# A hybrid decoder trunk on one Trainium2 core: the loads, row scales and last column pair of its first phase rearranged

## The reference, cut to what matters

```python
def rms_norm(t, gain):
    y = t32 * lax.rsqrt(jnp.mean(t32 * t32, axis=-1, keepdims=True) + NORM_EPS)
    return (y * gain).astype(t.dtype)

def modulate(h, shift, scale):
    return h * (1.0 + scale[:, None, :]) + shift[:, None, :]

c_act = jax.nn.silu(c)
mod = c_act @ ada_w[layer] + ada_b[layer]               # 2048 x 12288, six sections
h = modulate(rms_norm(x, norm_g[layer, 0]), shift_t, scale_t)
qkv = (h @ w_qkv).reshape(bsz, seq, N_A_GROUPS, 3, A_HEADS, HEAD_DIM)
q = apply_rope(rms_norm(qkv[:, :, g, 0], q_gain[g]), cos, sin)
```

## Time and profile before

| | |
|---|---|
| time before, median of 3 runs | 2384.81 us |
| lowest and highest | 2383.89 and 2385.09 us |
| span of the profiled execution, first to last instruction | 2381.5 us |
| mean granted TensorE clock | 0.998 |
| TensorE busy | 2340.9 us (98%) |
| VectorE busy | 1781.9 us (75%) |
| ScalarE busy | 1265.2 us (53%) |
| GpSimd busy | 52.8 us (2%) |
| moved by DMA | 665.38 MB, mean 279 GB/s |

### The profile page before, as it was taken

The page is one execution under the profiler, slowest core; times in us unless marked ns, Lnnn a source line. Parts: engine busy times, 40 slices in busy tenths (PEclk is TensorE's granted clock), DMA queues, the critical chain, the costliest instruction groups (busy, mean ns, idle before and its releaser), DMA issues.

```text
span 2381.5 us, 28881 instructions
## 1 busy us (share of the span) xinstructions
PE 2340.9 (98%) x11309; PEld 1933.7 (81%) x11309; DVE 1781.9 (75%) x2291; ACT 1265.2 (53%) x2162; POOL 52.8 (2%) x74
## 2 busy tenths in 40 slices
PE   7999999999999999999999999999999999999999
PEld 4478888887888888888887878877888888888887
DVE  6677888878999888789787887868875555555554
ACT  3166566667535535535546666654653553543552
POOL 1000000001000000000001210000100000000000
PEclk9999999999999999999999999999999999999999
DMA  9987888967999888898896877757886555555555
GB/s 391 424 324 288 320 296 311 359 220 256 356 390 345 336 307 327 299 337 315 315 350 224 324 305 249 264 179 288 302 282 194 189 192 194 186 194 193 187 191 172
DMA packets 151000, 665.38 MB, mean 279 GB/s; under 512 B 17392, under 2 KB 17872, under 8 KB 121424
## 3 DMA queue, kind: packets, MB, share of 16 engines
q1 hardware_dynamic: 150864, 663.53, 76.0%
HBM read 661.33 MB, written 2.13 MB: 279 GB/s over the span
## 4 chain that ended last, share of the span: by engine, by line
PE 82%; DMA 7%; DVE 6%; ACT 3%; issue 1%; POOL 1%; SPq 0%; ACTq 0%; DVEq 0%
PE main L512 18%; PE main L426 15%; PE main L428 15%; PE main L427 15%; PE main L514 9%; DMA qT<-ada 3%; DMA ada_raw<-ada 2%; DVE w_lo L1312 2%; DVE ada_raw L1319 2%; PE main L440 2%; PE main L442 2%; PE main L441 2%; DMA w_raw<-w 1%; ACT w_hi L885 1%; DVE qT L1319 1%
## 5 line engine op out<-in xcount | busy, mean ns | idle before, releaser
L885 ACT ACTIVATE w_hi<-w_raw 128x1024 fp32r<-128x1024 f32 x771 | 809.8, 1058 | 802.7 <-DMA w_raw<-w 798.6
L1312 DVE TENSOR_TENSOR w_lo<-w_raw,w_hi 128x1024 fp32r<-128x1024 f32 x771 | 933.9, 1224 | 398.1 <-ACT w_hi L885 392.0
L1319 DVE CUSTOM_DVE_ANT_0 ada_raw<-ada_raw,c_row,biasc 128x2048 f32<-128x2048 f32 x208 | 492.6, 2368 | 52.2 <-DMA ada_raw<-ada 50.4
L512 PE MATMUL main<-hT,w_hi 128*128 128x512 f32 x1856 | 464.7, 392 | 0.0
L512 PEld LDWEIGHTS main<-hT,w_hi 128*128 128x128 f32 x1856 | 334.3, 189 | 60.1
L426 PE MATMUL main<-w_hi,mid_hi 128*128 128x512 f32 x960 | 373.9, 389 | 1.0 <-DVE w_lo L1312 1.0
L427 PE MATMUL main<-w_lo,mid_hi 128*128 128x512 f32 x960 | 373.6, 389 | 0.0
L428 PE MATMUL main<-w_hi,mid_lo 128*128 128x512 f32 x960 | 373.5, 389 | 0.0
L426 PE MATMUL main<-w_hi,hT 128*128 128x512 f32 x848 | 338.9, 400 | 1.5 <-DVE hT L1478 1.0
L428 PE MATMUL main<-w_hi,hT 128*128 128x512 f32 x848 | 330.9, 390 | 0.0
L427 PE MATMUL main<-w_lo,hT 128*128 128x512 f32 x848 | 330.1, 389 | 0.0
(11 more groups left out here) (270 smaller groups left out, 1772.8 us busy)
## 6 DMA issues: line engine op xcount, KB each, us to landing
w_raw<-w SPq DMA_DIRECT2D x800, 512.0 KB, 4.3
ada_raw<-ada SPq DMA_DIRECT2D x208, 1024.0 KB, 7.1
qT<-ada SPq DMA_DIRECT2D x16, 1024.0 KB, 12.3
gate<-gate_rows SPq DMA_DIRECT2D x4, 1024.0 KB, 7.7
xs<-x SPq DMA_DIRECT2D x1, 2048.0 KB, 7.7
out<-xs SPq DMA_DIRECT2D x3, 512.0 KB, 6.7
out<-xs SPq DMA_DIRECT2D x2, 256.0 KB, 2.5
st_a<-lamb SPq DMA_DIRECT2D x1, 256.0 KB, 18.2
```

Source lines behind the costliest of these rows:

```text
L512: pe.matmul(banks[f][:, :], w_hi[:, s, wc], hT[:, :, kt, :], start=(kt == 0), stop=False)
L885: act.activation(w_hi[:, s, :], w_raw[:, s, :], ACT.Copy).then_inc(hi_done, 1)
L1312: dve.tensor_tensor(w_lo[:, s, :], w_raw[:, s, :], w_hi[:, s, :].bitcast(F32), ALU.subtract).then_inc(lo_done, 1)
L1319: dve.tensor_tensor_reduce(piece, piece, c_row[:, :], gain, biasc[:, section, kt:kt + 1], ALU.mult, ALU.add, out).then_inc(ada_used, 1)
```

## The change

1. The loads of `cols_in` and `biasc` are issued by ScalarE instead of SP, so that `x` is SP's first.
2. `x_recip` stands ahead of the second dot instead of behind it. ScalarE runs a square root on one element of `gate` early, between the exponential of `c` and its first copies.
3. One more weight piece is issued ahead of `pos_i` and `lamb`; every later one stands one place earlier. In the last pair's group the order is ada, w, ada, w, ada, w, ada, w, and two w follow.
4. In the last pair the four `ada` pieces are reordered: shift and scale of k-tile 14, then shift and scale of k-tile 15. ScalarE modulates and copies by k-tile (`last_high`), VectorE subtracts by k-tile (`last_low`), and TensorE runs all four parts for k-tile 14, then all four for k-tile 15 (`last_pair`).
5. The last two pieces of the seventh pair (j = 6) are multiplied in parts as well (`FIRST_EARLY` = 2).

```diff
 FIRST_SPLIT = 3
+FIRST_EARLY = 2
+FIRST_HALVES = PIECES + PK - 1
 ADA_QKV = [((g, c), j) for g, c, js in (
...
 
-            sp.dma_start(cols_in[0:96, :], vecs_in).then_inc(vec_in, 16)
-            sp.dma_start(biasc[:, :, :], bias_cols_in).then_inc(bias_in, 16)
             sp.dma_start(xs[:, :, :], x_in.rearrange("(t p) d -> p t d", p=P)).then_inc(x_in_done, 16)
...
                 first_ada(a)
+            weight_piece()
             weight_piece()
...
                     weight_piece()
-                for a in range(2, FIRST_PIECES):
-                    first_ada(FIRST_PIECES * j + a)
+                first_ada(FIRST_PIECES * j + 2)
+                if j == PIECES - 1:
+                    weight_piece()
+                first_ada(FIRST_PIECES * j + 3)
+                if j < PIECES - 1:
+                    weight_piece()
                 weight_piece()
-                weight_piece()
-            for _ in range(FIRST_CHUNKS - 1):
+            for _ in range(FIRST_CHUNKS - 2):
                 weight_piece()
...
                 banks = (main[0], main[1], (sc, ov), tr)[part]
-                if j == PIECES - 1 and part != first_order(j)[0]:
-                    pe.wait_ge(hT_split, PIECES)
+                if j == PIECES - 2 and part in first_order(j)[-FIRST_EARLY:]:
+                    pe.wait_ge(hT_split, j + 1)
                     s = next_piece()
                     for k in range(PK):
                         for t in range(T):
                             kt, tc, wc = PK * j + k, cols(t, P), cols(k, NC)
                             pe.matmul(banks[t][:, :], hT_hi[:, kt, tc], w_hi[:, s, wc], start=False, stop=False)
                             pe.matmul(banks[t][:, :], hT_hi[:, kt, tc], w_lo[:, s, wc], start=False, stop=False)
-                            last = pe.matmul(banks[t][:, :], hT_lo[:, kt, tc], w_hi[:, s, wc], start=False,
-                                             stop=(k == PK - 1))
+                            last = pe.matmul(banks[t][:, :], hT_lo[:, kt, tc], w_hi[:, s, wc], start=False, stop=False)
                     last.then_inc(mm_done, 1)
...
                         last = pe.matmul(banks[t][:, :], stb[:, j % 2, cols(k * T + t, P)], w_raw[:, s, cols(k, NC)],
-                                         start=(j == 0 and k == 0), stop=(j == PIECES - 1 and k == PK - 1))
+                                         start=(j == 0 and k == 0), stop=False)
                 last.then_inc(mm_done, 1)
+
+            def last_pair():
+
+                j = PIECES - 1
+                fills, raw = divmod(n["w"].n, SLOTS)
+                n["w"].up()
+                slots = [raw]
+                for k in range(PK):
+                    kt, wc = PK * j + k, cols(k, NC)
+                    for i, part in enumerate(first_order(j)):
+                        banks = (main[0], main[1], (sc, ov), tr)[part]
+                        if i == 0:
+                            pe.wait_ge(modulated, j + 1 + k)
+                            pe.wait_ge(raw_in[raw], 16 * (fills + 1))
+                            for t in range(T):
+                                last = pe.matmul(banks[t][:, :], stb[:, j % 2, cols(k * T + t, P)], w_raw[:, raw, wc],
+                                                 start=False, stop=(k == PK - 1))
+                        else:
+                            pe.wait_ge(hT_split, j + 1 + k)
+                            if k == 0:
+                                slots.append(next_piece())
+                            s = slots[i]
+                            for t in range(T):
+                                tc = cols(t, P)
+                                pe.matmul(banks[t][:, :], hT_hi[:, kt, tc], w_hi[:, s, wc], start=False, stop=False)
+                                pe.matmul(banks[t][:, :], hT_hi[:, kt, tc], w_lo[:, s, wc], start=False, stop=False)
+                                last = pe.matmul(banks[t][:, :], hT_lo[:, kt, tc], w_hi[:, s, wc], start=False,
+                                                 stop=(k == PK - 1))
+                        if k == PK - 1:
+                            last.then_inc(mm_done, 1)
 
             pe.wait_ge(c_ready, 1)
             spread_c()
             pe.wait_ge(turn_ready, 1)
             for j in range(PIECES):
                 first_transposes(j)
-            for j in range(PIECES):
+            for j in range(PIECES - 1):
                 for part in first_order(j):
                     first_piece(j, part)
-            n["split"].up(PIECES)
+            last_pair()
+            n["split"].up(FIRST_HALVES)
             h = (PIECES, hT_hi, hT_lo)
...
 
+            def last_high():
+
+                j = PIECES - 1
+                act.wait_ge(mm_done, SLOTS + FIRST_CHUNKS * (j - 1))
+                act.wait_ge(hT_split, j - 1)
+                for k in range(PK):
+                    dots(FIRST_PIECES * j + 2 * (k + 1))
+                    kt, part = PK * j + k, cols(k, T * P)
+                    g_col, s_col = (modc[:, x, kt:kt + 1] for x in (S_SCALE_T0, S_SHIFT_T0))
+                    act.activation(stb[:, j % 2, part], xnT[:, kt, :], ACT.Identity, bias=s_col,
+                                   scale=g_col).then_inc(modulated, 1)
+                    act.wait_ge(modulated, n["modulated"].up())
+                    act.activation(hT_hi[:, kt, :], stb[:, j % 2, part], ACT.Copy).then_inc(hi_part, 1)
+
+            act.dma_start(cols_in[0:96, :], vecs_in).then_inc(vec_in, 16)
+            act.dma_start(biasc[:, :, :], bias_cols_in).then_inc(bias_in, 16)
             act.wait_ge(eps_set, 1)
             act.activation(scratch_a[:, :], eps_t[:, :], ACT.Exp)
             act.wait_ge(vec_done, 1)
             act.activation(c_act[:, :], vec[:, V_C, :], ACT.Exp, scale=-1.0).then_inc(c_exp, 1)
+            act.activation(gate[:, 3, 0:1], eps_t[:, :], ACT.Sqrt)
             for q in range(2):
...
             q4, k4 = qT[:, 0:MAPS, :], kT[:, :, :]
-            act.sem_inc(hi_done, FIRST_CHUNKS * PIECES - FIRST_SPLIT)
-            n["w"].up(FIRST_CHUNKS * PIECES - FIRST_SPLIT)
+            unsplit = FIRST_CHUNKS * PIECES - FIRST_SPLIT - 1 - FIRST_EARLY
+            act.sem_inc(hi_done, unsplit)
+            n["w"].up(unsplit)
             for j in range(PIECES - 2):
                 keep_x(j)
-            for j in range(PIECES):
+            for j in range(PIECES - 1):
                 high(j, (S_SCALE_T0, S_SHIFT_T0), True)()
                 if j == 0:
                     keep_x(PIECES - 2)
                     keep_x(PIECES - 1)
                 if j == 1:
                     tables()
+            for _ in range(FIRST_EARLY):
+                split()
+            last_high()
+            act.sem_inc(hi_done, 1)
+            n["w"].up()
             for _ in range(FIRST_SPLIT):
...
                 dve.wait_ge(ada_start_in[s], 16 * (fills + 1))
-                dot(ada_start[s], (S_SHIFT_T0, S_SCALE_T0)[a // PK], PK * j + a % PK)
+                half, other = divmod(a, PK)
+                section, k = (other, half) if j == PIECES - 1 else (half, other)
+                dot(ada_start[s], (S_SHIFT_T0, S_SCALE_T0)[section], PK * j + k)
 
...
 
-            for j in range(PIECES):
+            def last_low(k):
+
+                kt = PK * (PIECES - 1) + k
+                dve.wait_ge(hi_part, n["hi"].up())
+                dve.tensor_tensor(hT_lo[:, kt, :], stb[:, (PIECES - 1) % 2, cols(k, T * P)], hT_hi[:, kt, :].bitcast(F32),
+                                  ALU.subtract).then_inc(hT_split, 1)
+
+            unsplit = FIRST_CHUNKS * PIECES - FIRST_SPLIT - 1 - FIRST_EARLY
+            dve.sem_inc(lo_done, unsplit)
+            n["w"].up(unsplit)
+            for j in range(PIECES - 1):
                 first_ada(j, 0)
                 if j == 0:
                     sum_x()
+                    x_recip()
                 else:
                     pair(j - 1, first=True)()
                 first_ada(j, 1)
-                if j == 0:
-                    x_recip()
                 first_ada(j, 2)
...
                     chained(dve.tensor_scalar(lam[:, 5:6], lam[:, 4:5], -LAM_INIT, None, ALU.add))
-            pair(PIECES - 1, first=True)()
-            dve.sem_inc(lo_done, FIRST_CHUNKS * PIECES - FIRST_SPLIT)
-            n["w"].up(FIRST_CHUNKS * PIECES - FIRST_SPLIT)
+            first_ada(PIECES - 1, 0)
+            pair(PIECES - 2, first=True)()
+            split()
+            first_ada(PIECES - 1, 1)
+            split()
+            first_ada(PIECES - 1, 2)
+            last_low(0)
+            first_ada(PIECES - 1, 3)
+            last_low(1)
+            dve.sem_inc(lo_done, 1)
+            n["w"].up()
             for _ in range(FIRST_SPLIT):
...
             arrive(4)
-            modulate_kept((S_SCALE_KV, S_SHIFT_KV), 4 * PIECES, 4 * GROUPS + 3)
+            modulate_kept((S_SCALE_KV, S_SHIFT_KV), FIRST_HALVES + 3 * PIECES, 4 * GROUPS + 3)
             n["hT"].up(PIECES)
...
```

(1 more changed line is left out.)

## The result

| | median | runs | ratio to before, 95% |
|---|---|---|---|
| before, same chip | 2384.63 us | 2383.89 to 2385.09, 5 | |
| changed | 2392.94 us | 2391.59 to 2395.73, 5 | 1.0035 [1.0024, 1.0045] |

The change makes the kernel slower by 8.3 us, 0.35%. The prediction was 2389.3 us, range 2384.7 to 2392.0: the sign was right, the size was not, and the result lies above the range. The profiled execution of the changed kernel took 2392.94 us, with a span of 2391.1 us.

The account below looks back on a forecast made before the run. The prediction took the full DMA stream to bound the first phase, TensorE most of the span. Release +5.0, start -0.5, all else 0 made +4.5 on 2384.8: 2389.3 us, range 2384.7 to 2392.0.

Parts of the forecast that it names:

- what bounds the phase: First 141 us: the DMA stream is full, 6.29 MB per pair in 14.80 us, and the period stays.
- parts 2 and 3: First phase: earlier row scales and one weight piece more ahead were each to gain 0.
- The rival on the other side: Pairs: TensorE's wait for part 3 goes unreplaced, 1.08 us in each of six pairs, 6.5 us; chance 0.06.
- part 4's mechanism and size: Last pair: splits wait behind the last dot's work, TensorE idles about 4 us, statistics start at 138.95, +5.0.
- the second wait: End of the phase: TensorE ends at 142.9 and waits 3.2 us for `main[0]`.
- the clock was taken to stay: Last pair: TensorE's new idle stretch of 4.1 us, shorter than the 4.6 us shown, was to cost no clock.
- the rival: Last pair: the clock falls in the new idle stretch, some 1.4 us lost, 2390.7 us; chance 0.15.
- the start: Kernel start: small loads by ScalarE let `x` issue earlier, gaining 0.5 us, bounds 0 to 0.91.
- The forecast for the last dot: Last pair: last ada piece lands at 127.13, less the 0.5 of part 1.
- the forecast 145.6: End of the phase: release of `main[0]`, put at 146.1 before the 0.5 us gained at kernel start.
- the shift of the release as the change of the total: From 141 us on: the release's shift passes whole to the total if nothing behind is DMA-bound; +4.5 us.
- the clock case: Range's upper end: clock falls in the last pair's idle stretch, no gain at kernel start, 2391.2 us; chance 0.15.

Follow-up runs that it names:

- Parts 1 to 3 alone: Kernel before with parts 1 to 3 of the change, last pair and its splits as before; 2384.90 us, ratio 1.0002.
- The order alone: Kernel before with part 4 only: last pair by k-tiles with its order of loads; 2389.04 us, ratio 1.0017.
- small loads back: Changed kernel with the loads of `cols_in` and `biasc` issued by SP again, ahead of `x`; 2393.57 us, ratio 1.0036.
- changed, again: The changed kernel itself, unaltered, timed and profiled a second time; 2394.96 us, ratio 1.0039.
- before, `lamb` late: Kernel before with the `lamb` broadcast load moved behind the gain loads, its operations into the first group; 2382.67 us, ratio 0.999.
- both waits filled: Changed kernel with float32 matmuls of a zero tile added in TensorE's first and second waits of the phase's end; 2389.92 us, ratio 1.0022.
- part 0 first: Changed kernel with part 0 of both k-tiles run before parts 3, 1 and 2 in the last pair; 2387.72 us, ratio 1.0012.

## Why the prediction was wrong

**Right: what bounds the phase, and parts 2 and 3.** The period stayed at 14.80, and the wait moved from part 3 to the modulation, at 0.8 us. Parts 1 to 3 alone measured -0.2 us in the medians, ratio 1.0002. The rival on the other side, a wait that nothing replaces, needed a period under 14.6; the starts of the changed kernel's last two plain pairs lie 14.77 apart (100.14, 114.91).

**Right: part 4's mechanism and size.** `w_lo` came 5.85 after the last dot (5.82), TensorE waited 3.96 (4.1), the release followed the statistics by 7.2 (7.15), the second wait was 3.15 (3.2). The order alone measured +4.0; by the prediction's steps it is the same +5.0 less the 1.23 us of the piece more ahead, 3.8. Moving part 0 alone took the excess from 8.3 to 2.6 us; 5.8 us of it show at the release, 1.7 of these by the clock that then doesn't fall.

**Wrong: the clock was taken to stay.** This is the step that failed. The prediction set 4.1 us of idling beside the 4.6 us after which the earlier trace rows show a clock below 1, and gave the fall a chance of 0.15. The fall came, behind 3.96 us. From 133.21 the three half pieces and part 0 took 7.68 us to the statistics where 6.0 were reckoned: 1.7 us, for which the rival had 1.4. Filling the wait gives it back. The error in the argument: the row showed when the clock had fallen in one long wait, and was read as if shorter waits were safe. Only waits behind which the clock held could say that, and once its first matmuls have run the trace of before has none between the 1.85 us near 1270 us and the 8.49 of the earlier trace rows. The runs have some: the clock held in the pair after 1.83, 1.49 and 1.24 us, and fell after 2.59, 3.96, 3.97 and 3.99 us (the last two in the second profile and with the small loads back). Filling the wait and nothing else kept the clock up, so the wait is the cause. The Trainium skill ("TensorE: Matmul & The Clock Gate", section "HAM oscillation — how this bites in real kernels") describes waits for a load between bursts of matmuls, behind which the clock falls every time. The traces agree for the wait near 4 us, in three profiles of three; behind the 3.15 us the clock fell in six of seven. The prediction gave the row more weight than it had.

**Wrong: one fall, where there can be two.** The wait of 3.15 us for `main[0]` was predicted to 0.05 us, but no rival asked what it does to the clock. Its cost by the marks is 0 to 0.9 us. The first profile has no second fall. In the second profile of the changed kernel the clock was low from 147.2 to 154.0; the rope's wait is gone there, having taken up its part of the loss, and the transposes behind it come 0.8 us later against the first group than in the first profile. Filling the wait took the excess from 7.2 to 5.2 us by the ratios, more than the marks explain; the intervals overlap.

**Mis-sized: the start.** The last dot was to start 0.5 us earlier than 127.13 and started at 127.36, 0.7 later than forecast. `x` landed at 8.8 instead of 9.4, so part 1 gave about the 0.5 that was reckoned, and something else takes it back. The trace gives each transfer 16 landing marks, one of each DMA engine. The time between the first mark and the last, read from them:

| | near 19 us | near 24 | near 40 | 100 to 122 |
|---|---|---|---|---|
| before | 0.7 | 2.1 | 2.1 | 2.1 |
| changed | 0.7 | 2.1 | 2.8 | 2.8 |
| changed, again | 0.5 | 1.8 | 2.9 | 3.0 |
| small loads back | 0.5 | 1.8 | 1.8 | 3.2 |
| before, `lamb` late | 0.7 | 1.0 | 2.1 (30 us) | 1.9 |

A piece counts as landed when all 16 parts are there, and the last of them falls 2 to 3 us behind, mostly in the first 45 us, and never catches up. The forecast for the last dot plus the lag beyond that of before gives 127.3 (changed), 127.5 (again) and 128.2 (small loads back, without the 0.5); measured are 127.36, 127.55 and 128.30. So the lag accounts for the 0.7 missing; no run changed it alone. What makes a part fall behind is open: it happens with `lamb` late too, only later, and the jumps sit at other times in other kernels, in the one of parts 1 to 3 alone at 79 us.

**The sum.** Release: +0.7 (lag), 0 (chain), +1.7 (clock), +0.1 (statistics) on the forecast 145.6 gives 148.1; measured 148.12. That is 2.5 of the 3.6 us by which the forecast was low. The remaining 1.1 lie behind the release, where the prediction put nothing: it took the shift of the release as the change of the total, having read TensorE's waits up to 260 us. If one counts TensorE's matmuls from the end, where the programs are the same, each one's start in the changed kernel less its start before is (the times are those of before):

| | at 233 us | 441 | 746 | 1237 | last |
|---|---|---|---|---|---|
| changed | 7.0 | 7.0 | 9.3 | 9.3 | 9.6 |
| changed, again | 7.9 | 7.9 | 8.9 | 8.9 | 10.2 |
| both waits filled | 5.9 | 5.9 | 10.0 | 10.0 | 9.8 |
| part 0 first | 1.2 | 1.2 | 1.4 | 1.4 | 0.6 |

So the profiled executions of changed and before differ by 7.0 us at the release and by 9.6 at the end, and 2.3 of the 2.6 between arise from 441 to 746 us, where TensorE waits in short pieces for `w_lo` and for attention's tiles (the DMA share in 560 to 750 us before is 0.94 to 0.96). The 1.1 is this 2.6 less the 1.5 us by which the profiled execution of before lay under its median. Two executions of the one changed kernel gain 2.3 and 0.9 us there, and the thirteen profiles 0 to 4.1; own time less the start of the first group runs from 2241.4 to 2246.8 us, with 2242.2 before (by the 1.85 us of own time beyond the span that the last section has). So this part differs between executions; how much of it the change itself brings, and what sets it, stays open.

**Ranges.** The upper end, 2392.0, was the clock case at the full price of the start and some tenths. The measured 2392.94 is 0.9 above it. The clock alone gives 2391.0 and with the lag 2391.7, both still inside; the 1.1 us behind the release takes it out. For the lag and for this last term the range had no allowance but "some tenths". (One sum of the prediction is off without effect: 114.7 + 6.86 + 5.44 is 127.0 and not 127.05.)

## What to carry to other kernels

When an order by k-tiles makes a chain's trigger wait for everything of its first k-tile, put what others wait for at its front: part 0 of both k-tiles first took the excess from 8.3 to 2.6 us here. A row that shows the clock fallen in a long wait does not make a shorter wait safe; give every new wait of TensorE of the length seen here (1.8 us and more, the shorter the less often) the possible price of a fall, up to 1.7 us, less what a later wait takes up, and look at each such wait along the whole chain, not at the first alone. Compare marks along the whole kernel too: here a quarter of the difference of the two profiles arose 300 us and more behind the change. In a phase bound by its transfers look at the stretches with a low rate before reordering anything: one broadcast load moved behind the phase gave 0.2 to 4.5 us, where the five parts of this change together gave nothing.

## What the runs showed of the hardware

- The clock fell after waits shorter than the prediction thought, 2.59 us in one case, and not at once: in that run at about 134.15 us, 0.9 us after TensorE had resumed. It stayed at 1.2 GHz from 133.15 to 136.56 in the first profile of the changed kernel, and from 147.2 (inside the second wait) to 154.0 in its other one; behind the same second wait it did not fall at all in the first. Behind the wait of 1.8 us near 1270 us it fell in five profiles of fourteen. Matmuls of zeros in the wait kept it up.
- A small load issued from ScalarE's queue at the same moment as a 2 MB load from SyncE's took 4.96 us for 48 KB; in front of it on SyncE's queue, it landed within 1.8 us of an issue at 0.74. The Trainium skill ("DMA: Bandwidth & Descriptors", section "Queues, rings and completion order") says that each DMA engine takes turns, packet by packet, between the queues that have work for it. The trace shows 3 us of delay; whether the large load beside it or the other queue makes it, no run here separates.
- One transfer's 16 parts land up to 3.4 us apart in the kernels of the table, and the lag grows in steps, most of them in the first 45 us.
- Own time less span was 1.85 us in the changed kernel's profile and the like in all other runs, where the prediction had taken 3.3 us from the median of before; by this the profiled execution of before took 2383.3 us, 1.5 less than its median.
